# HGRN heads: gate projections in pieces of two contraction tiles, and another order between heads

## The chip, the cores and the metric

The kernel runs on one core of a Trainium2 chip. The metric is device time in microseconds (us) for one execution. TensorE multiplies matrices into PSUM, which has eight banks; VectorE and ScalarE read the banks and work on SBUF; SyncE and GpSimd start the transfers of weights and constants. Each engine runs its own queue of instructions in order and waits on semaphores that the others raise.

## The reference

Two transformer blocks on 1024 tokens and 256 context tokens, 1024 wide, in float32. The edited stage is the HGRN branch of block 1, a gated linear recurrence in two directions with 4 heads of 128:

```python
def _hgrn_direction(q, f_logit, inp, lb, s0, reverse):
    f = lb + (1.0 - lb) * jax.nn.sigmoid(f_logit.astype(jnp.float32))
    log_f = _heads(jnp.log(f), HG_HEADS, HG_DIM)
    k = _heads(1.0 - f, HG_HEADS, HG_DIM)
    v = _heads(inp, HG_HEADS, HG_DIM)
    ...
    o, s = _gla_chunkwise(q, k, v, log_f, s0)

def _gla_chunkwise(q, k, v, log_f, s0):      # chunks of 32 tokens
    cum = jnp.cumsum(log_f, axis=3)
    u = jnp.einsum('bhnck,bhncv->bhnkv', k * jnp.exp(cum_last - cum), v)
    def step(state, inp):
        d, un = inp
        return d[..., None] * state + un, state
    ...
    qd = chunks(q) * jnp.exp(cum)
    scores = jnp.einsum('bhnck,bhnsk->bhncs', qd, k * jnp.exp(-cum))
    scores = jnp.where(lower_tri, scores, 0.0)
    o = (jnp.einsum('bhncs,bhnsv->bhncv', scores, v)
         + jnp.einsum('bhnck,bhnkv->bhncv', qd, s_start))
    ...
def _hgrn_readout(o, g_raw, norm_w, dtype):
    y = _rmsnorm(o, norm_w) * jax.nn.silu(g)
```

The gate logits of both directions, the query and the output gate are projections of the normalized tokens, each with a contraction over 1024.

## The kernel before, in words

The program is written out by hand, engine by engine; what stands in an engine's function is its order, and nothing schedules it anew. The stage is `hgrn`. It takes the heads one after the other.

**Fills.** A head needs ten projections, called fills (`fills`, n = 0 to 9). Fills 0 to 5 are the gates (`FG` is 6): two directions, each 256 context tokens and twice 512 tokens, so fills 0 and 3 are 256 wide and the others 512. Fills 6 and 7 are the query's two halves, 8 and 9 the output gate's. Each fill has eight contraction tiles (`KT` is 8), summed in one PSUM bank by `project` (L1590; the matmul is L1603). ScalarE's `store` empties the bank: gates with a sigmoid (L1680), query and output gate with a SiLU (L1682). `ps_full` counts fills that are done, `ps_free` fills that are stored. Float32 matmuls appear as two records each in the trace.

**Operands.** VectorE turns the sigmoids into forget gates (L1749), ScalarE takes their logarithms (L1703), VectorE sums them in chunks of 32 with a scan (L1755), ScalarE takes two exponentials (L1706, L1707), and VectorE makes the keys, the decays and the scaled query (L1759 to L1766). `q_rd` says that the operands stand; `chunks(h)` on TensorE waits for it.

**Steps.** `chunks(h)` (L1607) has 22 steps, s = 0 to 21, one for each tile of 128 tokens and direction, and two to finish. In step s TensorE transposes keys of tile s (L1616, bank 4), multiplies the keys of tile s-1 with the values (the updates, L1629, banks 0 to 3), makes the scores of tile s-1 (L1635, bank 5, from tile 4 on) and the outputs of tile s-2 (L1648, L1651, bank 6). ScalarE copies the turned keys out (L1717). VectorE advances the state four times (L1785), one after the other, masks the scores (L1797) and copies the outputs (L1806, L1809). The updates of a tile wait for the state of the tile before (`s_rd`).

**Gates ahead.** While head h is in its steps, TensorE also projects the gates of head h+1. `beside` says in which: one whole fill at the end of steps 2, 5, 8, 11, 14 and 17, always in bank 7. Head 1's first four gate fills are projected before head 0's steps. The other four fills of head h+1 follow after the last step. Then come the transposes of the head's normalized outputs (L1660), and the next head's steps.

**Between heads.** ScalarE sums the squares of the outputs (L1695), takes logarithm and exponential for the root (L1725, L1726), stores fills 6 and 7 of the next head, and then takes the logarithms of its gates. VectorE scales the outputs (L1811), makes the forget gates, and goes on to the scans; `gated` (L1740) multiplies the turned outputs with the output gate. A change between sigmoid, SiLU, logarithm and exponential puts a table load on ScalarE.

Of the kernel before, what the change touches and what calls it, by code (L numbers as in the profile page):

```python
# [20 lines left out]
P = 128  # L21
# [1497 lines left out]
def hgrn(pg):  # L1519
# [40 lines left out]
    r_sq = pg.shared_sem("norm_squares", HEADS * T // P)  # L1560
# [3 lines left out]
    AHEAD = FH + 4  # L1564

    def bank_of(h, n):

        if FH * h + n < AHEAD:
            return (f0 + FH * h + n) % 8
        return 7 if n < FG else 2 + n - FG  # L1570

    def beside(h):

        todo = range(AHEAD - FH if h == 0 else 0, FG)
        return {3 * i + 2: n for i, n in enumerate(todo)}
# [13 lines left out]
    def tensor(e):  # L1589
        def project(h, which):  # L1590
            for n in which:
                part, (t, a, b) = fills[n]
                f = f0 + FH * h + n
                if f < f0 + AHEAD:
                    pg.bank_free(e, f)
                elif n < FG:
                    e.wait_ge(pg.ps_free, f)
                elif n == FG:
                    e.wait_ge(s_rd, 20 * h)
                    e.wait_ge(sm_rd, 16 * h)  # L1600
                slot = pg.weights(e, g0 + 2 * h + part)
                for k in range(KT):
                    mm = e.matmul(pg.ps[:, bank_of(h, n), 0:b - a], slot[:, (2 * k + t) * P:(2 * k + t + 1) * P],  # L1603
                                  h1[:, k, a:b], start=(k == 0), stop=(k == KT - 1))
                mm.then_inc(pg.ps_full, 1)

        def chunks(h):  # L1607
            e.wait_ge(pg.ps_free, f0 + max(FH * (h + 1), AHEAD))
            e.wait_ge(q_rd, 2 * h + 2)
            for s in range(2 * NT + 2):  # L1610
                if s < 2 * NT:
                    k, d = divmod(s, 2)
                    t = tile_of(k, d)
                    if h or s:
                        e.wait_ge(k_cp, 20 * h + s)
                    e.transpose(pg.ps[:, 4, 0:P], A[:, 2 * (h % 2) + d, t * P:(t + 1) * P], pg.ident).then_inc(t_rd, 1)  # L1616
                if 1 <= s <= 2 * NT:
# [9 lines left out]
                    for c in range(4):  # L1627
                        r = slice(C * c, C * c + C)
                        mm = e.matmul(pg.ps[:, c, 0:P], KT_[r, E % 4, :], V[r, t, h * P:(h + 1) * P], start=True, stop=True)  # L1629
                    mm.then_inc(u_rd, 1)  # L1630
                    if k >= 2:
                        L = 16 * h + u - 4
                        if L:
                            e.wait_ge(sm_rd, L)
                        e.matmul(pg.ps[:, 5, 0:P], Cn[:, d, t * P:(t + 1) * P], B[:, d, t * P:(t + 1) * P],  # L1635
                                 start=True, stop=True).then_inc(sc_rd, 1)
                if s >= 2:
# [3 lines left out]
                    if k >= 2:  # L1641
# [3 lines left out]
                        if L:  # L1645
                            e.wait_ge(o_cp, L)
                        bank = pg.ps[:, 6, 0:P]
# [10 lines left out]
            r_sc.wait(e, h + 1)  # L1658
            for t in range(T // P):
                mm = e.transpose(pg.ps[:, t // 4, (t % 4) * P:(t % 4 + 1) * P], YT[:, t, :], pg.ident)  # L1660
            mm.then_inc(y_turned.sem, 1)

        project(0, range(FH))
        project(1, range(AHEAD - FH))
# [3 lines left out]
    def scalar(e):  # L1668
# [28 lines left out]
        store(0, range(FH))  # L1697
        for h in range(HEADS):
            if h:
                store(h, [FG + 1])  # L1700
# [7 lines left out]
            if h:  # L1708
                store(h, range(FG + 2, FH))
            else:  # L1710
                store(1, range(AHEAD - FH))
            for s in range(2 * NT):
# [5 lines left out]
                if h + 1 < HEADS and s - 1 in beside(h):  # L1718
                    store(h + 1, [beside(h)[s - 1]])
                if s - 4 >= 12:  # L1720
                    square(h, s - 4)
            for s in range(2 * NT - 4, 2 * NT):
# [3144 lines left out]
```

## Time and profile before

| | us |
|---|---|
| median of 3 runs | 3565.79 |
| lowest, highest | 3562.51, 3567.89 |
| span of the profiled execution | 3560.1 |
| HGRN stage in it, first projection to last gated output | 425.5 to 900.2 |

The profiled execution is a further one; its span runs from its first to its last instruction. In a timeline a row is a run of equal instructions: its start, how long it lasted, engine, line, operation, and in brackets the idle time of the engine before it and what ended it. `PE` is TensorE's matmuls, `DVE` VectorE, `ACT` ScalarE. The end of a matmul is modelled, so starts are the safer numbers. `PEclk` is the clock granted to TensorE, 1.00 for 2.4 GHz and 0.50 for 1.2 GHz.

### The profile page before, as it was taken

Reading aid. Unit: us, or ns where it says so; the run is one execution under the profiler, and the core shown is the slowest. Engines: PE = TensorE matmul, PEld = TensorE weight load, DVE = VectorE, ACT = ScalarE, POOL = GpSimd, SP = SyncE. Lnnn points to the kernel's source line nnn. Section 1 sums busy time; section 2 is a strip of 40 time slices with the busy share of each in tenths; the row PEclk is TensorE's granted clock in tenths of the full one; section 3 lists DMA queues with packets and bytes.
Section 4 is the critical chain, followed back from the end, with each engine's and each line's share of the span. In section 5 each row is a group of like instructions: output and inputs, shape, how many; then the busy total and the mean of one; then the engine's idle time right before and its main releaser. Section 6 shows DMA issues by size and latency. Waiting matters only on the chain. (4 is left out here: it accounts for less than half of the span.)

```text
span 3560.1 us, 38398 instructions
## 1 busy us (share of the span) xinstructions
PE 3274.5 (92%) x15060; PEld 2447.1 (69%) x15060; DVE 1885.4 (53%) x2863; ACT 1217.0 (34%) x1887; POOL 657.4 (18%) x616
## 2 busy tenths in 40 slices
PE   7999998988899999999998998888968899999997
PEld 4476544444678778888887777665456678888785
DVE  6546626446323374443476734445675376555558
ACT  3325623212422253333233333451220243333344
POOL 3100000000100025544001010001000015555433
PEclk8899999996899999999999999998989899999998
DMA  5430000000333232222766123233224133222765
GB/s 227 172 130 13 10 24 24 13 13 1 121 117 104 96 104 80 86 83 87 288 247 258 43 65 93 90 97 125 60 107 154 59 103 110 97 105 101 256 241 171
DMA packets 124763, 389.24 MB, mean 109 GB/s; under 512 B 15751, under 2 KB 33159, under 8 KB 109352
## 3 DMA queue, kind: packets, MB, share of 16 engines
q1 hardware_dynamic: 86872, 267.32, 21.8%
q0 software_dynamic: 21056, 111.05, 8.4%
q10 hardware_dynamic: 16656, 8.42, 1.3%
q8 instruction: 120, 1.97, 0.2%
q14 instruction: 59, 0.48, 0.0%
HBM read 312.17 MB, written 74.58 MB: 109 GB/s over the span
## 5 line engine op out<-in xcount | busy, mean ns | idle before, releaser
L1603 PE MATMUL banks<-work,weight_ring 128*128 128x512 f32 (+1 forms) x640 | 263.8, 573 | 0.5 <-ACTq L4685 0.5
L2185 POOL TENSOR_TENSOR quad_raw<-quad_raw 128x512 f32<-128x512 f32 x160 | 234.7, 1468 | 124.1 <-DMA quad_raw<-in_w_gu 117.9
L2317 PE MATMUL banks<-block_t_high,quad_low 128*128 128x512 f32 x608 | 236.5, 389 | 0.0
L1603 PEld LDWEIGHTS banks<-work,weight_ring 128*128 128x128 f32 x640 | 126.3, 200 | 129.2 <-issue 123.8
L1785 DVE SCALAR_TENSOR_TENSOR x<-x,work,banks 128x128 f32<-128x128 f32 x320 | 111.3, 348 | 137.9 <-PE banks L1629 127.4
L2470 ACT ACTIVATE quad_partial<-banks 128x512 f32<-128x512 f32 x160 | 95.6, 598 | 241.3 <-PE banks L2317 236.6
L2315 PE MATMUL banks<-block_t_high,quad_high_b 128*128 128x512 f32 x456 | 177.5, 389 | 0.2 <-ACT quad_partial L2470 0.2
L2316 PE MATMUL banks<-block_t_low,quad_high_b 128*128 128x512 f32 x456 | 177.4, 389 | 0.0
L2317 PE MATMUL banks<-block_b_high,quad_low 128*128 128x512 f32 x456 | 177.4, 389 | 0.0
L3331 PE MATMUL banks<-mix_high,ring_parts 128*128 128x512 f32 x320 | 135.0, 422 | 13.2 <-ACT work L3390 4.5
L2556 DVE TENSOR_TENSOR quad_gated<-banks,quad_partial 128x512 f32<-128x512 f32 x40 | 27.7, 692 | 214.8 <-PE banks L2317 211.2
L2661 PE MATMUL banks<-hidden_high,pair_high 128*128 128x512 f32 x352 | 137.4, 390 | 1.5 <-DVE x L2720 1.5
L2663 PE MATMUL banks<-hidden_high,pair_low 128*128 128x512 f32 x352 | 136.9, 389 | 0.0
L2662 PE MATMUL banks<-hidden_low,pair_high 128*128 128x512 f32 x352 | 136.9, 389 | 0.0
L2317 PEld LDWEIGHTS banks<-block_t_high,quad_low 128*128 128x128 f32 x608 | 114.2, 188 | 23.6
L3332 PE MATMUL banks<-mix_low,ring_parts 128*128 128x512 f32 x320 | 129.2, 404 | 0.0
L3333 PE MATMUL banks<-mix_high,ring_parts 128*128 128x512 f32 x320 | 128.9, 403 | 0.0
L2235 DVE TENSOR_TENSOR quad_low<-quad_raw,quad_high_a 128x1536 fp32r<-128x1536 f32 x44 | 84.9, 1928 | 77.5 <-POOL quad_raw L2185 76.1
L1872 POOL DMA_DIRECT2D branches<-work x32 | 17.4, 543 | 555.1 <-ACT work L1943 552.8
L2315 PE MATMUL banks<-block_b_high,quad_high_a 128*128 128x512 f32 x304 | 118.3, 389 | 0.0
L2316 PE MATMUL banks<-block_b_low,quad_high_a 128*128 128x512 f32 x304 | 118.3, 389 | 0.0
L2235 DVE TENSOR_TENSOR quad_low<-quad_raw,quad_high_b 128x2048 fp32r<-128x2048 f32 (+1 forms) x44 | 94.3, 2143 | 34.1 <-ACT quad_high_b L2224 34.1
(650 smaller groups left out, 8174.6 us busy)
## 6 DMA issues: line engine op xcount, KB each, us to landing
quad_raw<-in_w_gu SPq DMA_DIRECT2D x40, 768.0 KB, 4.3
condition_space<-in_mod_w POOLq DMA_DIRECT2D x24, 1024.0 KB, 6.9
pair_raw<-in_w_down SPq DMA_DIRECT2D x22, 1024.0 KB, 5.4
down_raw<-in_w_down SPq DMA_DIRECT2D x33, 512.0 KB, 4.5
columns_raw<-ffn_blocks SPq DMA_DIRECT2D x33, 512.0 KB, 5.6
weight_ring<-in_w_merge SPq DMA_DIRECT2D x24, 512.0 KB, 3.8
quad_raw<-in_w_gu SPq DMA_DIRECT2D x48, 256.0 KB, 3.1
weight_ring<-in_dft SPq DMA_DIRECT2D x12, 1024.0 KB, 5.0
```

The lines of the kernel that those rows point to most:

```text
L1603: mm = e.matmul(pg.ps[:, bank_of(h, n), 0:b - a], slot[:, (2 * k + t) * P:(2 * k + t + 1) * P], h1[:, k, a:b], start=(k == 0), stop=(k == ...
L2185: e.tensor_tensor(self.weight(n, out), self.weight(n, a), self.weight(n, b), op).then_inc(self.sums.sem, 1)
L2235: e.tensor_tensor(flat(pg.w_low[n % 2][:, a:b]), pg.w_raw[n % 2].big[:, a * HALF:b * HALF], flat(high).bitcast(F32), ALU.subtract).then_in ...
L2315: e.matmul(bank, w_hi[:, k], hi[:, k], start=(start and k == 0), stop=False, skip_group_check=again)
L2316: e.matmul(bank, w_hi[:, k], lo[:, k], start=False, stop=False, skip_group_check=again)
L2317: mm = e.matmul(bank, w_lo[:, k], hi[:, k], start=False, stop=(k == 3), skip_group_check=again)
L2661: e.matmul(bank, wh[:, k, m], hh[:, k], start=(p == 0 and k == 0), stop=False)
L2662: e.matmul(bank, wh[:, k, m], hl[:, k], start=False, stop=False)
L2663: mm = e.matmul(bank, wl[:, k, m], hh[:, k], start=False, stop=(p == NP - 1 and k == 1))
L3331: e.matmul(bank, w_hi[:, c], MH[:, k, t], start=start, stop=False)
L3332: e.matmul(bank, w_hi[:, c], ML[:, k, t], start=False, stop=False)
L3333: mm = e.matmul(bank, w_lo[:, c], MH[:, k, t], start=False, stop=stop)
```

## The change

It has four parts.

- **Gates in pieces.** `beside` becomes a list with one entry for each of the 22 steps: two contraction tiles of a 512-wide gate fill, or four of a 256-wide one, behind the outputs of the step. The six gate fills end with step 19. Steps 20 and 21 take four tiles each of fill 6.
- **The start.** Head 1's first four gate fills are no longer projected before head 0's steps, and `chunks` no longer waits for all stores.
- **Banks and order on TensorE.** Fill 6 goes to bank 4, fill 7 to bank 7, fills 8 and 9 to banks 5 and 6. The output transposes move between fill 7 and fill 8.
- **Between heads.** ScalarE takes the next head's gate logarithms right behind the logarithm of the root, ahead of the root's exponential, and stores fills 6 to 9 behind the exponentials. VectorE makes the next head's forget gates (and clears the first states) ahead of the scaling, and does `gated` of the last head ahead of the two query products.

```diff
-    AHEAD = FH + 4
+    BANK = (7, 7, 7, 7, 7, 7, 4, 7, 5, 6)
+    STEPS = 2 * NT + 2
...
-        todo = range(AHEAD - FH if h == 0 else 0, FG)
-        return {3 * i + 2: n for i, n in enumerate(todo)}
+    def in_steps():
+
+        out, finished = [], {}
+        for n in range(FG + 1):
+            _, (_, a, b) = fills[n]
+            each = 4 if n == FG or b - a < HALF else 2
+            for k in range(0, KT, each):
+                finished[n] = len(out)
+                out.append([(n, j) for j in range(k, k + each)])
+        return out, finished
+
+    beside, finished = in_steps()
...
+            for n, k in todo:
                 part, (t, a, b) = fills[n]
                 f = f0 + FH * h + n
...
+                if k == 0:
+                    if n == 0 and h:
+                        e.wait_ge(pg.ps_free, f - 2)
+                    elif n < FG and h == 0:
+                        if n >= 4:
+                            e.wait_ge(pg.ps_free, f - 3)
+                    elif 0 < n < FG:
+                        e.wait_ge(pg.ps_free, f)
+                    elif n == FG and h:
+                        e.wait_ge(k_cp, 20 * h)
+                    elif n == FG + 1 and h:
+                        e.wait_ge(pg.ps_free, f - 1)
+                    elif n == FG + 2 and h:
+                        e.wait_ge(sm_rd, 16 * h)
+                    elif n == FG + 3 and h:
+                        e.wait_ge(o_cp, 16 * h)
...
-            e.wait_ge(pg.ps_free, f0 + max(FH * (h + 1), AHEAD))
             e.wait_ge(q_rd, 2 * h + 2)
...
-                if h + 1 < HEADS and s in beside(h):
-                    project(h + 1, [beside(h)[s]])
+                if h + 1 < HEADS:
+                    project(h + 1, beside[s])
             if h + 1 < HEADS:
-                project(h + 1, range(FG, FH))
...
-        project(0, range(FH))
-        project(1, range(AHEAD - FH))
+                project(h + 1, all_of([FG + 1]))
+            turn_outputs(h)
+            if h + 1 < HEADS:
+                project(h + 1, all_of([FG + 2, FG + 3]))
+
+        project(0, all_of(range(FH)))
...
+        store(0, range(FG))
+        gate_logs(0)
+        for h in range(HEADS):
             for d in range(2):
                 e.wait_ge(c_rd, 2 * h + d + 1)
                 e.activation(Cn[:, d, :], B[:, d, :], ACT.Exp, scale=-1.0).then_inc(n_rd, 1)
                 e.activation(B[:, d, :], B[:, d, :], ACT.Exp).then_inc(e_rd, 1)
-            if h:
-                store(h, range(FG + 2, FH))
-            else:
-                store(1, range(AHEAD - FH))
+            store(h, range(FG, FH))
...
+                if h + 1 < HEADS:
+                    store(h + 1, [n for n in range(FG) if finished[n] == s - 1])
```

Three places show the new order. TensorE, from the end of head 0's tail into head 1's steps. Before (L1660 the output transposes, L1616 key transposes, L1629 updates, L1603 projection):

```order
L1603 MATMUL banks<-work,weight_ring 128x512 x32
L1660 MATMUL banks<-parameters,work 128x128 x8
L1616 MATMUL banks<-parameters,x 128x128 x2
L1629 MATMUL banks<-work,x 128x128 x4
L1616 MATMUL banks<-parameters,x 128x128
L1629 MATMUL banks<-work,x 128x128 x4
L1603 MATMUL banks<-work,weight_ring 128x256 x8
```

After (L1631 the output transposes, L1643 key transposes, L1656 updates, L1620 projection):

```order
L1620 MATMUL banks<-work,weight_ring 128x512 x12
L1631 MATMUL banks<-parameters,work 128x128 x8
L1620 MATMUL banks<-work,weight_ring 128x512 x16
L1643 MATMUL banks<-parameters,x 128x128
L1620 MATMUL banks<-work,weight_ring 128x256 x4
L1643 MATMUL banks<-parameters,x 128x128
L1656 MATMUL banks<-work,x 128x128 x4
L1620 MATMUL banks<-work,weight_ring 128x256 x4
L1643 MATMUL banks<-parameters,x 128x128
L1656 MATMUL banks<-work,x 128x128 x4
L1620 MATMUL banks<-work,weight_ring 128x512 x2
```

The transposes now stand inside the tail's projections, and a piece of projection stands in every step, from step 0 on.

ScalarE between heads 0 and 1. Before (L1725 and L1726 the root, L1682 the stores of query and output gate, L1703 the gate logarithms, L1706 and L1707 the exponentials):

```order
L1725 ACT_TABLE_LOAD
L1725 ACTIVATE work<-work,parameters 128x8
L1726 ACT_TABLE_LOAD
L1726 ACTIVATE work<-work 128x8
L1682 ACT_TABLE_LOAD
L1682 ACTIVATE work<-banks 128x512 x2
L1703 ACT_TABLE_LOAD
L1703 ACTIVATE work<-x 128x1280 x2
L1706 ACT_TABLE_LOAD
```

After (L1755 and L1759 the root, L1730 the gate logarithms, L1737 and L1738 the exponentials):

```order
L1755 ACT_TABLE_LOAD
L1755 ACTIVATE work<-work,parameters 128x8
L1730 ACTIVATE work<-x 128x1280 x2
L1759 ACT_TABLE_LOAD
L1759 ACTIVATE work<-work 128x8
L1737 ACTIVATE work<-work 128x1280
L1738 ACTIVATE work<-work 128x1280
```

The gate logarithms stand two table loads and two stores earlier; the four stores (L1712) follow together behind the exponentials.

VectorE at the same place. Before (L1811 the scaling, L1749 forget gates, L1755 scan):

```order
L1811 TENSOR_TENSOR work<-work 128x1024
L1749 TENSOR_SCALAR x<-x,parameters 128x1280 x2
L1755 SCALAR_TENSOR_TENSOR work<-work 128x1280
L1756 TENSOR_SCALAR x<-x 128x1280
```

After (L1780 forget gates, L1782 clearing, L1850 the scaling, L1791 scan):

```order
L1780 TENSOR_SCALAR x<-x,parameters 128x1280 x2
L1782 MEMSET x 128x128 x2
L1850 TENSOR_TENSOR work<-work 128x1024
L1791 SCALAR_TENSOR_TENSOR work<-work 128x1280
L1792 TENSOR_SCALAR x<-x 128x1280
```

The forget gates no longer stand behind the scaling, and with it behind the root.

## Rows read from the trace of the kernel before

**Rows 1.** Stretches: us, busy of PE, PEld, DVE, ACT, POOL, PEclk, DMA share, GB/s.
```profile
603.60:718.00 114.40, 99.27 (x540) 53.85 (x540) 54.54 (x132) 29.88 (x61) 0.00 (x0) 0.93 0.06 19
...
833.10:900.20 67.10, 53.42 (x380) 33.77 (x380) 39.95 (x119) 11.39 (x40) 0.00 (x0) 0.50 0.00 1
```

**Rows 2.** Timeline, TensorE, steps of head 1: start, us, work, [idle before].
```profile
668.48 0.50 PE L1629 MATMUL banks<-work,x 32*128 32x128 f32 x8 [0.45 <-ACT x L1717]
...
669.91 7.13 PE L1603 MATMUL banks<-work,weight_ring 128*128 128x512 f32 x16
...
677.08 0.50 PE L1629 MATMUL banks<-work,x 32*128 32x128 f32 x8
...
679.30 0.50 PE L1629 MATMUL banks<-work,x 32*128 32x128 f32 x8 [0.46 <-ACT x L1717]
```

**Rows 3.** Timeline, TensorE, end of head 1, starts of heads 2 and 3.
```profile
684.85 27.73 PE L1603 MATMUL banks<-work,weight_ring 128*128 128x512 f32 x64
712.42 1.04 PE L1660 MATMUL banks<-parameters,work 128*128 128x128 f32 x8
718.04 0.45 PE L1616 MATMUL banks<-parameters,x 128*128 128x128 f32 x1 [4.58 <-issue]
...
833.07 0.45 PE L1616 MATMUL banks<-parameters,x 128*128 128x128 f32 x1 [4.57 <-issue]
```

**Rows 4.** Timeline, ScalarE, between heads 1 and 2.
```profile
685.73 1.28 ACT L1725 ACT_TABLE_LOAD   x1
...
687.35 1.28 ACT L1726 ACT_TABLE_LOAD   x1
...
700.80 2.43 ACT L1703 ACTIVATE work<-x 128x1280 f32<-128x1280 f32 x2
```

**Rows 5.** Timeline, VectorE, between heads 1 and 2.
```profile
688.88 1.23 DVE L1811 TENSOR_TENSOR work<-work 128x1024 f32<-128x1024 f32 x1 [3.60 <-ACT work L1726]
690.02 1.80 DVE L1749 TENSOR_SCALAR x<-x,parameters 128x1280 f32<-128x1280 f32 x2
702.10 2.83 DVE L1755 TENSOR_TENSOR_SCAN work<-work 128x1280 f32<-128x1280 f32 x1 [10.28 <-ACT work L1703]
...
717.85 1.40 DVE L1740 SCALAR_TENSOR_TENSOR work<-banks,parameters,work 128x512 f32<-128x512 f32 x2
```

**Rows 6.** Timeline, start of the stage: ScalarE, TensorE.
```profile
460.15 0.60 ACT L1680 ACTIVATE x<-banks 128x512 f32<-128x512 f32 x1 [6.27 <-PE banks L1603]
...
508.69 0.33 PE L1616 MATMUL banks<-parameters,x 128*128 128x128 f32 x1 [0.47 <-ACT x L1680]
```

**Rows 7.** Timeline, all engines, a step early in head 1.
```profile
614.25 0.27 PE L1616 MATMUL banks<-parameters,x 128*128 128x128 f32 x1
...
614.56 0.28 ACT L1717 ACTIVATE x<-banks 128x128 f32<-128x128 f32 x1 [8.03 <-PE banks L1616]
614.86 1.28 ACT L1680 ACT_TABLE_LOAD   x1
614.89 0.33 PE L1616 MATMUL banks<-parameters,x 128*128 128x128 f32 x1
...
616.15 0.38 ACT L1680 ACTIVATE x<-banks 128x256 f32<-128x256 f32 x1
```

**Rows 8.** Busy time by stretch, columns as in rows 1.
```profile
757.00:760.00 3.00, 2.45 (x31) 1.75 (x32) 2.27 (x9) 0.28 (x1) 0.00 (x0) 0.99 0.01 3
760.00:763.00 3.00, 3.00 (x16) 2.12 (x16) 1.66 (x6) 0.00 (x0) 0.00 (x0) 0.50 0.03 5
763.00:766.00 3.00, 3.00 (x14) 2.42 (x13) 0.00 (x0) 0.00 (x0) 0.00 (x0) 0.94 0.00 0
```

**Rows 9.** Timeline, VectorE, two state steps of head 3.
```profile
862.37 1.50 DVE L1785 SCALAR_TENSOR_TENSOR x<-x,work,banks 128x128 f32<-128x128 f32 x4 [0.86 <-PE banks L1629]
...
865.25 1.50 DVE L1785 SCALAR_TENSOR_TENSOR x<-x,work,banks 128x128 f32<-128x128 f32 x4 [0.86 <-PE banks L1629]
```

**Rows 10.** Timeline, TensorE, the fourth gate fill within head 2's steps.
```profile
761.33 4.70 PE L1603 MATMUL banks<-work,weight_ring 128*128 128x256 f32 x16
```

More of the change, by code:

```diff
@@ L1589, in tensor, with project @@
     def tensor(e):
-        def project(h, which):
-            for n in which:
+        def project(h, todo):
+            for n, k in todo:
                 part, (t, a, b) = fills[n]
                 f = f0 + FH * h + n
[L1594 to L1600, printed above, removed]
-                slot = pg.weights(e, g0 + 2 * h + part)
[L1602 to L1605, printed above, removed]
+                if k == 0:
[14 more added lines that the diff above has]
+                        e.wait_ge(o_cp, 16 * h)
+                slot = pg.weights(e, g0 + 2 * h + part)
+                mm = e.matmul(pg.ps[:, bank_of(h, n), 0:b - a], slot[:, (2 * k + t) * P:(2 * k + t + 1) * P],
+                              h1[:, k, a:b], start=(k == 0), stop=(k == KT - 1))
+                if k == KT - 1:
+                    mm.then_inc(pg.ps_full, 1)
@@ L1607, in chunks, with all_of, turn_outputs @@
+        def all_of(which):
+            return [(n, k) for n in which for k in range(KT)]
+        def turn_outputs(h):
+            r_sc.wait(e, h + 1)
+            for t in range(T // P):
+                mm = e.transpose(pg.ps[:, t // 4, (t % 4) * P:(t % 4 + 1) * P], YT[:, t, :], pg.ident)
+            mm.then_inc(y_turned.sem, 1)
         def chunks(h):
-            e.wait_ge(pg.ps_free, f0 + max(FH * (h + 1), AHEAD))
             e.wait_ge(q_rd, 2 * h + 2)
-            for s in range(2 * NT + 2):
+            for s in range(STEPS):
@@ L1628, in chunks @@
                         r = slice(C * c, C * c + C)
-                        mm = e.matmul(pg.ps[:, c, 0:P], KT_[r, E % 4, :], V[r, t, h * P:(h + 1) * P], start=True, stop=True)
+                        mm = e.matmul(pg.ps[:, c, 0:P], KT_[r, E % 4, :], V[r, t, h * P:(h + 1) * P],
+                                      start=True, stop=True)
                     mm.then_inc(u_rd, 1)
@@ L1695, in square, with gate_logs @@
             e.activation(junk, YT[:, t, :], ACT.Square, accum_out=ss[:, t:t + 1]).then_inc(r_sq.sem, 1)
-        store(0, range(FH))
-        for h in range(HEADS):
-            if h:
-                store(h, [FG + 1])
+        def gate_logs(h):
             for d in range(2):
@@ L1742, in gated, with forget_gates @@
             ins.then_inc(done, 1)
-        for h in range(HEADS):
-            a = [A[:, 2 * (h % 2) + d, :] for d in range(2)]
+        def forget_gates(h):
             e.wait_ge(pg.ps_free, f0 + FH * h + FG)
@@ L1748, in vector @@
                 i = 4 * d + h
-                e.tensor_scalar(a[d], a[d], pg.one_minus_lb[:, i:i + 1], pg.lb[:, i:i + 1], ALU.mult,
-                                ALU.add).then_inc(f_rd, 1)
+                a = A[:, 2 * (h % 2) + d, :]
+                e.tensor_scalar(a, a, pg.one_minus_lb[:, i:i + 1], pg.lb[:, i:i + 1], ALU.mult, ALU.add).then_inc(f_rd, 1)
+            for d in range(2):
+                ch(e.memset(S[:, 8 * d, :], 0.0))
+        forget_gates(0)
+        for h in range(HEADS):
+            a = [A[:, 2 * (h % 2) + d, :] for d in range(2)]
             for d in range(2):
```

50 lines of the change are left out of this document (26 added, 24 removed).

## The prediction

> **What bounds the kernel now.** The busy table and the chain that ended last cannot answer this: the chain ends long after the edited stage. I read the stage cut at each head's first transpose, then the timelines of TensorE, ScalarE and VectorE inside one head, looking at each place for the wait that ends last. A middle head takes 114.4 us, of which TensorE is busy 99.3 at a mean granted clock of 0.93; the last head, without projections, runs at 0.50, the lower of the clock's two levels [rows 1]. Within a head two regimes alternate [rows 2]. A step with no projection is a loop between two engines: updates on TensorE, four chained state steps on VectorE, updates again. It takes 2.20 us and TensorE idles 0.46 of it (677.08 to 679.30). A step that carries a whole gate fill takes 8.60 us (668.48 to 677.08) and is all TensorE; VectorE idles there. So the idle 0.46 is never filled, since the next projection tile is behind a step boundary. Between heads there is a third regime. After the last outputs (684.85, call it E) TensorE projects four fills in 27.57 us, but the next head starts only at 718.04, E + 33.2 [rows 3]: ScalarE stores two query fills first, then loads the logarithm table, and takes the gates' logarithms at E + 15.95 [rows 4], and VectorE's scans start at E + 17.25 [rows 5]. TensorE has nothing to do for the last 4.6 us.
>
> **The start of the stage.** TensorE projects ten fills of head 0 and four of head 1 before the first chunk step at 508.69 [rows 6]. Now the first chunk waits for its ten alone. A wide fill is 27.57 / 4 = 6.89 us at full clock [rows 3], a narrow one half; the four that go are 6.89 x 2 + 3.45 x 2 = 20.7, and the 0.47 in which TensorE waited for the last store goes too. Head 0 then starts at 487.5, **21.2 us earlier**, if its operands are ready. They are: ScalarE has the sixth gate at 460.8 [rows 6], table, logarithm and scan put the scan at about 463.5, and 17.1 us after a scan starts (below) the operands stand, at about 481.
>
> **The steps.** Every step now carries two 512-wide tiles (four narrow ones), 4 x 0.43 = 1.72 us by 6.89 / 8 for each tile. The step with eight tiles took 8.60; six tiles fewer leave 8.60 - 5.17 = 3.43 us, one switch between small matmuls and projection included [rows 2, 3]. That is above the 2.20 of the loop, so TensorE sets the pace and does not idle. There are 14 such steps (6 to 19): 48.0 us. Steps 0 to 5 have no outputs: a transpose and updates are 0.64 us [rows 7], with the tiles 2.4; step 0 about 2.0, step 5 with its scores 2.7. Step 2 has a wait of its own. Fill 1 goes into bank 7, which ScalarE must have emptied of fill 0, and ScalarE's first sigmoid of a head needs a table load. In the trace the same copy, load and store stand at 614.56, 614.86 and 616.15: the next instruction could start about 2.2 us after the transpose at 614.25, where the tiles were due after 0.64 [rows 7]. So step 2 costs about 3.95. The later handovers of bank 7 are free: ScalarE's copy and a 0.60 store end about 1.1 us after a transpose, the tiles are due 1.6 after it (0.20, and then the 1.43 from 668.48 to 669.91 [rows 2]). Steps 0 to 5: 2.0 + 3 x 2.4 + 3.95 + 2.7 = 15.9. Step 20 has updates, scores, outputs and four tiles, 1.43 + 3.45 = 4.9, step 21 its outputs, 0.75. With the odd tenths of waits for semaphores I take **70.0 us** from a head's start to E.
>
> What the single bank costs is bounded below by nothing (all hidden) and above by the 1.6 at step 2 plus about 1 us at each of the five other handovers.
>
> The Trainium skill, page "Perfetto Trace Analysis", Optimizing Tensor Performance, Matmuls, speaks against this change there: independent matmul groups should rotate through different PSUM banks, so that the evacuation of one overlaps the next. By that rule all six handovers of a head are open, some 7 us in a head instead of 1.6. The rows agree with it for step 2 alone.
>
> **Between heads.** TensorE after E: the last four tiles of fill 6 (3.45), fill 7 (6.89), eight transposes (about 0.95), fills 8 and 9 (13.78): 25.1 us. The other engines: ScalarE loads the logarithm table at E + 0.88, and where it loaded the exponential's it now starts the gates' logarithms, E + 2.50, for 2.43 [rows 4]. VectorE's forget gates, put ahead of the scaling, take 1.80 [rows 5] and are ready by E + 2.3, under the first load. From the start of the second load to VectorE's scaling were 1.53 us (687.35 to 688.88); now that makes E + 6.46. It lasts 1.23, overlapping the next a little; the scans, now queued behind it, start at E + 7.6, not 17.25 [rows 5]. From the first scan to the operands were 15.75 us (702.10 to 717.85); the gated output of the head before, 1.40, now stands ahead of the two query products: 17.1, so operands at E + 24.7 and the head's start at E + 24.9. The two paths end within 0.2 us of each other; TensorE's is later, **25.1 in place of 33.2**. The output transposes need the scaling, done at E + 7.7, and are reached at E + 10.4: no wait. The query stores wait behind the exponentials until about E + 18, still ahead of the products that need them (E + 22.3). The last store (fill 9) delays the head's first key copy by about 0.4 us, under step 0's tiles. SyncE's loads keep their order, and each slot is free 25 us or more before its next use.
>
> **The sum.** A head is 70.0 + 25.1 = 95.1. Heads 0 to 2 from 487.5: head 3 starts at 772.8, where it started at 833.07 [rows 3]: 60.3 us earlier. Head 3 has no projection, and I let it take as long as before. Against the 60.3 stands the clock. Before, TensorE idles 4.6 us in front of a head [rows 3], and behind head 3's pause comes half clock [rows 1]; that pause goes, and the sum uses full-clock rows. But a head keeps one sparse place, the 1.6 us wait in step 2. After 757 to 760, where only small matmuls ran, the clock fell; from 760 to 763 it was at half, with small matmuls up to 761.33 and projection behind them, and from 763 it was 0.94 [rows 8, 10]. I allow 2.3 us for one or two such dips. **Forecast: 58 us less**, a span of 3502, and against the median of 3565.8 (5.7 above the span) 3507.8 us.
>
> **Rivals.** *The clock falls in the steps and stays down; slower.* A small-matmul step at half clock takes 2.88 us [rows 9], and two tiles there 3.44: 6.3 in place of 3.43, 2.9 more. It decides from about 20 of the 66 steps. If it starts in step 3 and lasts to E in all three heads, it costs 19 x 3 x 2.9 = 165, or about 150 us, since some steps hold less: 3658; in one head alone about 50, 3558. For it: in head 3 TensorE is busy without pause at half clock and the clock never rises, and its array now sees small matmuls for half of every step. Against it: the dip at 760 ended with such a mix [rows 8, 10]. 8%, of which 5% slower.
>
> The Trainium skill, page "TensorE: Matmul & The Clock Gate", section "HAM oscillation — how this bites in real kernels", asks for all contraction tiles of one output in one run, so that TensorE's clock stays up. That is a rule against splitting the contraction over the steps, and by it the time is this rival's, above 3600. The trace agrees only for steps without any projection.
>
> *The handovers are all open.* If ScalarE's stores come late at each, 5 x 1 us in three heads: +15, 3523. 8%.
>
> *Head 3 keeps full clock*, since no pause precedes it: 15 to 16 steps of 2.20 for 2.88, 10.5 us less: 3497. Against it: its first steps hold only small matmuls, and from 757 to 760 such steps brought the clock down [rows 8]. 7%.
>
> *The order between heads brings nothing*, because a wait that I don't see (the root's table, the scaling) holds the scans as long as before: 3 x 8 = 24 back, 3532. 4%.
>
> **The numbers.** The forecast has 73%, with its own range 3500 to 3516. The range 3494 to 3527 takes in open handovers and the fast head 3, and leaves 12% out. What a measurement of this kernel can tell from no change is about 0.2%, 7 us. Faster 0.92, same 0.03 (one head at half clock), slower 0.05.
>
> **What would show it.** Right: head 0's first chunk transpose near 487.5; updates 3.43 apart in steps 6 to 19; 95 us between heads' starts; scans 7.6 us after E; TensorE without a gap ahead of each head; one gap of 1.6 us in step 2; granted clock near 1.0 in heads 0 to 2. Wrong: a clock of 0.5 across steps with projection, updates 6.3 apart, gaps at each change of fill, or a pause of TensorE between the last fill and the next head.

## The result, and the profile after

| | before | after |
|---|---|---|
| median of the runs, us | 3566.84 (3562.51 to 3578.63, 4 runs) | 3506.81 (3504.79 to 3508.18, 4 runs) |
| span of the profiled execution, us | 3560.1 | 3506.1 |
| ratio of the times, 95% interval | 1 | 0.9827 (0.9806 to 0.9848) |
| heads' first transposes, us | 508.7, 603.6, 718.0, 833.1 | 487.7, 582.9, 678.1, 773.2 |
| end of the stage, us | 900.2 | 839.6 |
| from there to the end, us | 2659.8 | 2666.4 |

The changed kernel is faster by 60 us than the kernel before on the same chip. The forecast was 3507.8 us; the median is 3506.8.

The stretches of the profile after, cut at the heads' starts and at the stage's end as in [rows 1] (us; busy time of PE, PEld, DVE, ACT, POOL; granted clock; DMA share; GB/s):

```profile
487.69:582.87 95.18, 93.55 (x542) 49.42 (x540) 54.34 (x131) 25.79 (x58) 0.00 (x0) 1.00 0.07 23
582.87:678.05 95.18, 93.55 (x542) 49.42 (x541) 54.43 (x131) 25.80 (x58) 0.00 (x0) 1.00 0.07 23
678.05:773.22 95.17, 93.54 (x541) 49.42 (x540) 54.35 (x131) 25.80 (x58) 0.00 (x0) 1.00 0.03 12
773.22:839.60 66.38, 52.17 (x381) 33.09 (x379) 38.44 (x115) 11.87 (x41) 0.00 (x0) 0.53 0.00 1
839.60:3506.00 2666.40, 2481.02 (x11068) 1980.08 (x11068) 1403.95 (x1801) 909.93 (x1304) 594.68 (x499) 0.96 0.36 125
```

A middle head took 114.40 us with TensorE busy 99.27 at a clock of 0.93 [rows 1]. Now it takes 95.18 with TensorE busy 93.55 at 1.00. The matmuls are the same, so of the 19.2 us 5.7 were busy time, lost to the lower clock, and 13.5 were idle time. The last head, which has no projection beside it, is nearly as it was: clock 0.53 (0.50 before), 66.4 us to the end of the stage (67.1 before).

The same stretch from the stage's end to the kernel's end in the profile of before, same columns:

```profile
900.20:3560.00 2659.80, 2473.43 (x11068) 1973.20 (x11068) 1408.20 (x1801) 909.87 (x1304) 598.69 (x499) 0.96 0.37 125
```

It has the same instructions (11068 matmuls) and took 6.6 us less. That is why the two spans are 54 us apart and the stage 60.6. It isn't a cost of the change: the changed kernel profiled a second time (below) took 2657.6 there.

The stage's first fill, before and then after. Before, 14 fills stand ahead of head 0's first transpose at 508.69 [rows 6]; after, ten stand ahead of 487.69:

```profile
425.47 82.75 PE L1603 MATMUL banks<-work,weight_ring 128*128 128x256 f32 x224 [0.52 <-ACTq L4685]
425.75 62.11 PE L1620 MATMUL banks<-work,weight_ring 128*128 128x256 f32 x160 [0.52 <-ACTq L4724]
```

From its first fill to head 0 the stage took 83.2 us before and takes 61.9 now, 21.3 less. The whole stage, from its first fill, took 474.7 us and takes 413.8, 60.9 less.

TensorE in the first steps of head 0, and three steps with outputs (start, us, work, [idle before]), against [rows 2, 6, 7]:

```profile
487.69 0.27 PE L1643 MATMUL banks<-parameters,x 128*128 128x128 f32 x1
487.80 1.89 PE L1620 MATMUL banks<-work,weight_ring 128*128 128x256 f32 x8
...
492.20 0.50 PE L1656 MATMUL banks<-work,x 32*128 32x128 f32 x8
494.33 1.98 PE L1620 MATMUL banks<-work,weight_ring 128*128 128x512 f32 x4 [1.63 <-ACT x L1710]
...
507.40 0.50 PE L1656 MATMUL banks<-work,x 32*128 32x128 f32 x8
...
508.83 1.98 PE L1620 MATMUL banks<-work,weight_ring 128*128 128x512 f32 x4
...
510.86 0.50 PE L1656 MATMUL banks<-work,x 32*128 32x128 f32 x8
```

Updates (L1656) are 3.45 us apart, and TensorE does not idle: every such step has the same shape, where before one step of 8.60 us followed on steps of 2.20. The only gap is in step 2, where fill 1 waits for ScalarE's copy out of bank 7 (L1710). It is the only one in each of the three heads with projection: a head's 95.18 us less 93.55 of busy time is 1.63. The line of costly groups on the profile's page says the same, since 3 x 1.63 = 4.9; the other 0.5 of its 5.4 us stands in front of the stage's first fill:

```profile
L1620 PE MATMUL banks<-work,weight_ring 128*128 128x512 f32 (+1 forms) x640 | 265.0, 560 | 5.4 <-ACT x L1710 4.9
```

Between heads 0 and 1, TensorE, then VectorE, then ScalarE, against [rows 3, 5, 4]. The last outputs end at E = 557.86:

```profile
557.86 10.57 PE L1620 MATMUL banks<-work,weight_ring 128*128 128x512 f32 x24
568.26 1.04 PE L1631 MATMUL banks<-parameters,work 128*128 128x128 f32 x8
569.13 13.90 PE L1620 MATMUL banks<-work,weight_ring 128*128 128x512 f32 x32
582.87 0.27 PE L1643 MATMUL banks<-parameters,x 128*128 128x128 f32 x1
```

```profile
558.20 1.80 DVE L1780 TENSOR_SCALAR x<-x,parameters 128x1280 f32<-128x1280 f32 x2
...
564.27 1.23 DVE L1850 TENSOR_TENSOR work<-work 128x1024 f32<-128x1024 f32 x1 [3.88 <-ACT work L1759]
565.41 2.82 DVE L1791 TENSOR_TENSOR_SCAN work<-work 128x1280 f32<-128x1280 f32 x1
...
580.20 2.35 DVE L1805 SCALAR_TENSOR_TENSOR work<-work 128x1024 f32<-128x1024 f32 x2
```

```profile
558.73 1.28 ACT L1755 ACT_TABLE_LOAD   x1
560.03 0.30 ACT L1755 ACTIVATE work<-work,parameters 128x8 f32<-128x8 f32 x1
560.24 2.41 ACT L1730 ACTIVATE work<-x 128x1280 f32<-128x1280 f32 x2
562.67 1.28 ACT L1759 ACT_TABLE_LOAD   x1
```

TensorE works without a gap from the last outputs to the next head's first transpose, E + 25.0, where it stood still for the last 4.6 us of 33.2 [rows 3]. The logarithms (L1730) share the root's table and need no load of their own, and the scans start at E + 7.55 instead of E + 17.25 [rows 5]. VectorE has the operands at 582.55, 0.3 before TensorE is done with its projection: the two paths end together.

### The profile page after: what moved, and what is told of

The parts are those of the page before. It is cut to its first block and busy times, and to the rows that moved or that the text cites. A ratio compares the mean times of both kernels' runs of the same rounds, so it can differ in the third digit from the quotient of the medians.

```text
span 3506.1 us, 38398 instructions
## 1 busy us (share of the span) xinstructions
PE 3262.6 (93%) x15060; PEld 2438.4 (70%) x15060; DVE 1879.7 (54%) x2863; ACT 1203.9 (34%) x1878; POOL 653.3 (19%) x616
## 5 line engine op out<-in xcount | busy, mean ns | idle before, releaser
L1620 PE MATMUL banks<-work,weight_ring 128*128 128x512 f32 (+1 forms) x640 | 265.0, 560 | 5.4 <-ACT x L1710 4.9
L1620 PEld LDWEIGHTS banks<-work,weight_ring 128*128 128x128 f32 x640 | 115.9, 190 | 115.0 <-issue 104.5
L2951 PE MATMUL banks<-down_high 128*128 128x512 f32 x264 | 103.9, 394 | 6.8 <-DVE down_low L3023 3.6
```

The source lines that it names most:

```text
L2951: e.matmul(bank, wh[:, c], bh, start=first, stop=False)
```

## The experiments

Every ratio is to the kernel before on the same chip, with its 95% interval. What runs ahead of the stage differs by some us between executions: head 0 starts at 485.7 to 490.2 in kernels with the same beginning, and at 482.2 and 482.6 in two more, though in each of these the stage's first fill is 61.9 us ahead of it. So I compare lengths: the stage from head 0's first transpose to the gated output of head 3 (351.9 us in the changed kernel), a head's cycle (95.18), from its start to E (70.2 to 70.3) and from E to the next start (25).

### Whole fills again, the rest of the change kept

Six gate fills of the next head go whole into steps 2, 5, 8, 11, 14 and 17; each is stored one step later.

```
-        out, finished = [], {}
+        out, finished = [[] for _ in range(STEPS)], {}
-        for n in range(FG + 1):
-            _, (_, a, b) = fills[n]
-            each = 4 if n == FG or b - a < HALF else 2
-            for k in range(0, KT, each):
-                finished[n] = len(out)
-                out.append([(n, j) for j in range(k, k + each)])
+        for n in range(FG):
+            finished[n] = 3 * n + 2
+            out[finished[n]] = [(n, j) for j in range(KT)]
+        for i in range(2):
+            out[2 * NT + i] = [(FG, j) for j in range(4 * i, 4 * i + 4)]
...
-            if h + 1 < HEADS:
-                store(h + 1, [FG - 1])
```

> The changed kernel (3506.8 us) with one part undone: the gate fills are whole again, in steps 2, 5, 8, 11, 14 and 17, in bank 7; the early start and the order between heads stay. Theory (the pieces fill TensorE's idle time in every step): a group of three steps takes 13.0 us instead of 3 x 3.46 = 10.4, so a head's way to its last outputs grows from 70.1 us to 81 to 84, +33 to +42 in three heads: 3540 to 3549. Rival (the gain is that of the start and of the order between heads, since TensorE was 87% busy in a middle head anyway): +15 at most, under 3522.

Measured: 3536.13 us (3535.74 to 3540.77), 0.9904 (0.9883 to 0.9924), 4 us under the range expected. The stage took 388.2 us, 36.3 more than with the pieces, which was expected; from a head's start to E it was 81.8, 80.5 and 84.9 us, against 70.2. The three heads, and TensorE over one period of three steps in head 1:

```profile
485.71:592.43 106.72, 96.88 (x542) 52.86 (x540) 54.34 (x131) 25.70 (x58) 0.00 (x0) 0.97 0.06 20
592.43:697.79 105.36, 95.52 (x541) 51.76 (x540) 54.41 (x131) 25.70 (x58) 0.00 (x0) 0.98 0.06 21
697.79:807.53 109.74, 99.89 (x541) 54.52 (x540) 54.44 (x131) 25.70 (x58) 0.00 (x0) 0.94 0.03 10
```

```profile
642.53 7.13 PE L1618 MATMUL banks<-work,weight_ring 128*128 128x512 f32 x16
...
654.12 0.50 PE L1654 MATMUL banks<-work,x 32*128 32x128 f32 x8 [0.45 <-ACT x L1743]
...
655.55 7.13 PE L1618 MATMUL banks<-work,weight_ring 128*128 128x512 f32 x16
```

A period of three steps takes 13.02 us (642.53 to 655.55). Three steps of the changed kernel take 10.35, but they hold six tiles of 512 columns and the period holds eight, which by 0.86 us a tile is 1.72 of the difference; so the two are not to be compared as they stand, as the expectation does. The loop's latency is the rest: in the two steps without projection TensorE waits 0.45 us in front of the updates. A whole head has the same matmuls in both kernels. There TensorE idles 9.8 us instead of 1.6 (in head 1, 5.0 in four waits for VectorE's states, 4.1 in nine for the key copies), which makes 24.6 us in three heads. The rest, a third of the 36.3, is the clock, which dips six times, each time beginning between two whole fills or before a head's first: TensorE's busy time is 3.3, 2.0 and 6.4 us longer than in the changed kernel, 11.7 of the 36.3. So the pieces are worth 29 us by the medians (27 by the ratios) and 36 by the stage, and they pay by giving each step something to do, not by less work.

### Logarithms behind the exponential and two query stores, as before

```
-            store(h, range(FG, FH))
+            store(h, range(FG + 2 if h else FG, FH))
...
-            if h + 1 < HEADS:
-                gate_logs(h + 1)
             e.wait_ge(r_lg, h + 1)
             e.activation(ss, ss, ACT.Exp, scale=-0.5).then_inc(r_rt.sem, 1)
+            if h + 1 < HEADS:
+                store(h + 1, [FG, FG + 1])
+                gate_logs(h + 1)
```

> The changed kernel with ScalarE's order between heads undone: root's logarithm, root's exponential, stores of fills 6 and 7, and only then the gates' logarithms; all else stays. Theory (VectorE's scans wait for these logarithms and then set the next head's start): the scans start near E + 13.6 instead of E + 7.6 (E is the end of the last outputs), the next head at E + 31 instead of E + 25; 3 x 5.8 = +17, and TensorE's pause of 5 to 6 us in front of each head brings half clock in its first steps, up to 4 us each: 3524 to 3537. Rival (TensorE's own path of 25.1 us hides them): 0 to +3, at most 3510.

Measured: 3527.17 us (3519.48 to 3532.34), 0.9877 (0.9853 to 0.9901); the stage took 374.4 us, 22.5 more. TensorE in front of head 1 (E = 560.35), and VectorE's first scan:

```profile
571.63 13.90 PE L1620 MATMUL banks<-work,weight_ring 128*128 128x512 f32 x32
591.38 0.47 PE L1643 MATMUL banks<-parameters,x 128*128 128x128 f32 x1 [5.85 <-DVE work L1806]
591.64 3.62 PE L1620 MATMUL banks<-work,weight_ring 128*128 128x256 f32 x8
```

```profile
574.17 2.83 DVE L1792 TENSOR_TENSOR_SCAN work<-work 128x1280 f32<-128x1280 f32 x1 [8.50 <-ACT work L1730]
```

The scan is at E + 13.8, the head's start at E + 31.0 instead of 25.0. The pause also triggers something: the clock is at half from 589.0 and again from 691.4, for 6.8 us each (the eight matmuls in 3.62 us, against 1.89 in the changed kernel), and heads 1 and 2 are about 2 us longer to E. The cycles are 6.0, 8.2 and 7.8 us longer, and the pause is 6.0 of each. The two parts, 36.3 + 22.5 = 58.8 us, come near to the 60.9 by which the whole stage is shorter.

### Four fills of head 1 ahead of the first head

They use banks 0 to 3, as head 0's did, and their stores stand ahead of head 0's first key copy, as before the change; `chunks(0)` waits for all stores again (these edits are left out below).

```
         project(0, all_of(range(FH)))
+        project(1, all_of(range(4)))
...
-                    project(h + 1, beside[s])
+                    project(h + 1, [v for v in beside[s] if h or v[0] >= 4])
```

> The changed kernel with the start undone: head 1's first four gate fills are projected before head 0's steps again (banks 0 to 3), and steps 0 to 11 of head 0 carry no projection. Theory (a step without projection cannot take less than the 2.2 us of the loop between TensorE and VectorE, so work taken out of the steps gives back only part): start +21.2, steps 0 to 5 about -4, steps 6 to 11 6 x (3.46 - 2.20) = -7.6, together +9 to +10, with a dip of the clock up to +14: 3516 to 3521. Rival (the early start is worth its whole 21 us): 3528.

Measured: 3523.65 us (3514.56 to 3527.39), 0.9865 (0.9842 to 0.9888). That is 2.7 us over the range expected. The first chunk starts at 507.37, and head 0 is shorter only by 3.7 us, so the stage, from its first fill, is 17.6 us longer. The expectation takes 11.6 us off head 0, which makes 58.6 us to E; it took 66.6. The 17.6 can't be added to the 36.3 and 22.5 of the two runs above, since the four fills moved here are pieces in head 0's steps too. The stretches of head 0:

```profile
507.37:509.80 2.43, 1.35 (x11) 0.72 (x11) 0.84 (x3) 0.83 (x3) 0.00 (x0) 1.00 0.00 0
509.80:543.90 34.10, 28.71 (x188) 17.39 (x189) 19.57 (x61) 2.77 (x10) 0.00 (x0) 0.50 0.00 1
543.90:598.87 54.97, 54.97 (x279) 27.02 (x278) 34.67 (x68) 18.80 (x39) 0.00 (x0) 1.00 0.06 20
```

```profile
540.37 3.74 PE L1622 MATMUL banks<-work,weight_ring 128*128 128x512 f32 x4
```

Steps 0 to 11 hold small matmuls alone. TensorE fell to the lower clock 2.4 us into them, was busy 28.71 of 34.10 us there, and came back to the upper clock at 543.9, within the first two projection tiles (from 540.37). So work done ahead is not free even where it only moves: here it left twelve steps to the lower clock, and the step that brought it back is one with projection.

Small matmuls alone don't bring the clock down everywhere, though. Head 0 of the kernel before has no projection behind step 5 either, and there such steps kept the upper clock for 33 us, after the whole fill in step 5:

```profile
540.00:550.00 10.00, 7.78 (x94) 5.09 (x94) 8.01 (x28) 1.39 (x5) 0.00 (x0) 1.00 0.04 13
550.00:560.00 10.00, 8.22 (x97) 5.34 (x97) 8.20 (x28) 1.40 (x6) 0.00 (x0) 1.00 0.01 2
```

So the same steps stand at both levels in these traces. The clock fell at the start of a head that has nothing but small matmuls there, in steps without scores and outputs, in which TensorE waits 1.3 to 1.5 us for VectorE; but it fell in later steps too, at 760 in the trace before [rows 8] and at 748 in the run with whole fills, where it held in the rows above. What decides between these, no run shows.

### Pauses put into the steps

To try the slower rival, ScalarE holds the key copy back once in each of heads 0 to 2, by 26 small copies, so that TensorE stands still in the middle of steps with two tiles.

```
+                if h < 3 and s == 7 + h:
+                    for _ in range(26):
+                        pg.achain(e)(e.activation(junk, pg.ident, ACT.Copy))
                 e.activation(KT_[:, E % 4, :], pg.ps[:, 4, 0:P], ACT.Copy).then_inc(k_cp, 1)
```

> The changed kernel with a pause of TensorE put into the steps of heads 0, 1 and 2: ScalarE does 26 idle copies ahead of the key copy of step 7, 8 and 9, about 9 us of work of which 3 are hidden, so TensorE stands still for about 6 us in each. Theory (half of each step is dense projection, and that brings the clock back): behind each pause the clock falls to half and is back within about 10 us, which costs 2 to 5 us: 3506.8 + 3 x 6 + 3 x 3.5 = 3535 (3528 to 3545). Rival (with small matmuls in half of each step the clock stays down until the head's tail): 12 steps x 2.9 = 35 us more in each head, 3625 or more.

Measured, in one run: 3527.65 us, beside 3571.08 of before (median of that chip). One run is not enough to judge the time (it lies just under the range expected), but the trace answers the question. TensorE behind the pause of head 0, and the stretches with their clocks:

```profile
515.13 0.47 PE L1643 MATMUL banks<-parameters,x 128*128 128x128 f32 x1 [5.89 <-ACT x L1748]
...
518.01 3.00 PE L1620 MATMUL banks<-work,weight_ring 128*128 128x512 f32 x4
...
522.48 1.98 PE L1620 MATMUL banks<-work,weight_ring 128*128 128x512 f32 x4
```

```profile
513.30:520.10 6.80, 4.97 (x24) 2.89 (x25) 1.89 (x6) 1.90 (x7) 0.00 (x0) 0.50 0.00 0
520.10:530.00 9.90, 9.90 (x80) 6.13 (x80) 4.94 (x17) 1.32 (x4) 0.00 (x0) 1.00 0.01 2
```

The clock fell to half in each pause and was back 6.8, 10.2 and 6.8 us after it fell. It never stayed down: a head cost 8.3 to 9.4 us more, of which the pause is 5.9. The rival that gives 3558 to 3658 us needs it to stay down for whole heads, and is refuted for steps of this shape, half small matmuls and half projection. Together with the run above: once down, the clock stayed at half for 34 us without the projection tiles, and for 7 to 10 with them.

### Another bank for the first fill

The trace shows one handover of bank 7 that is not hidden, the first of a head. Here fill 0 goes into bank 5, whose other user (the scores) comes later.

```
-    BANK = (7, 7, 7, 7, 7, 7, 4, 7, 5, 6)
+    BANK = (5, 7, 7, 7, 7, 7, 4, 7, 5, 6)
...
-                        e.wait_ge(pg.ps_free, f - 2)
+                        e.wait_ge(pg.ps_free, f - 1)
...
-                    elif 0 < n < FG:
+                    elif 1 < n < FG:
...
-                            e.wait_ge(pg.ps_free, f0 + FH * h + FG + 3)
+                            e.wait_ge(pg.ps_free, f0 + FH * (h + 1) + 1 if h + 1 < HEADS else f0 + FH * h + FG + 3)
```

> The changed kernel with fill 0 of the next head in bank 5 instead of 7: bank 5 is first used by the scores of step 5, so fill 1 can start in bank 7 in step 2 without waiting for the table load and the store of fill 0. Theory: the only wait of TensorE in a head, 1.63 us in step 2, goes, 3 x 1.63 = 4.9 us less than the changed kernel's 3506.8: 3502 (3500 to 3504). Rival (another wait takes its place: the key copy of step 3 stands behind the table load too, and TensorE needs it in step 4): no change, 3506 to 3508.

Measured: 3498.03 us (3489.66 to 3503.26), 0.9803 (0.9785 to 0.9821). TensorE at the same place, where the changed kernel waits 1.63 us:

```profile
493.52 0.50 PE L1656 MATMUL banks<-work,x 32*128 32x128 f32 x8
493.95 1.98 PE L1620 MATMUL banks<-work,weight_ring 128*128 128x512 f32 x4
```

The wait is gone, a head's cycle is 93.48 instead of 95.18, and nothing else came late in its place: 3 x 1.70 = 5.1 us in the stage. The stage took 346.5 us, 5.4 less. By the ratios the whole is 8.6 us below the changed kernel's, though the two did not run side by side; 4.9 were expected, and the stage shows 5.4.

### Head 3 kept at the upper clock by extra matmuls

Head 3 gets matmuls that compute nothing anyone reads, into bank 7, where the other heads have their projection. They are work on top of the reference's.

```
                 if h + 1 < HEADS:
                     project(h + 1, beside[s])
+                else:
+                    for n in (512, 256) if s < 5 else (128,):
+                        e.matmul(pg.ps[:, 7, 0:n], pg.ident, h1[:, 0, 0:n], start=True, stop=True)
```

> The changed kernel with idle matmuls in head 3, which has no projection (identity times tokens, into bank 7, read by nobody): a 512-wide and a 256-wide one in steps 0 to 4, a 128-wide one in each later step. Theory (head 3 runs at half clock only because its first steps leave TensorE idle for most of the time): the clock stays at its upper level, steps take 2.2 to 2.3 us instead of 2.88, and the merge behind starts at full clock: 10 to 13 us less, 3494 to 3497. Rival (small matmuls bring the clock down whatever stands between them): the clock falls, and the idle matmuls cost up to 0.3 us a step: 3507 to 3513.

Measured: 3502.0 us (3493.63 to 3508.15), 0.9807 (0.9791 to 0.9824). Head 3 of the changed kernel after its first 4.2 us, and head 3 with the extra matmuls:

```profile
777.40:839.60 62.20, 50.19 (x361) 32.02 (x360) 36.92 (x111) 10.55 (x37) 0.00 (x0) 0.50 0.00 1
```

```profile
775.64:824.40 48.76, 42.71 (x427) 27.68 (x425) 34.26 (x112) 9.82 (x38) 0.00 (x0) 1.00 0.01 1
```

With more matmuls on TensorE (427 in 48.76 us) the head is shorter: 46.9 us from its start to its last outputs instead of 57.7. The mechanism works, and the stage is 10.8 us shorter (341.1). But the time is not: against the changed kernel it is 5 us less by the medians, with intervals that overlap, where 10 to 13 were expected. The stages behind it took 2674.8 us in this execution, the slowest of its five. The expectation also wanted the next stage to start at full clock. It does not: TensorE waits 4.8 us for the scaled outputs behind the head, and the clock falls again, at 824.4, before the stage ends at 831.2:

```profile
824.40:831.20 6.80, 1.97 (x8) 1.56 (x8) 2.61 (x3) 2.05 (x4) 0.00 (x0) 0.50 0.00 0
```

Which of the extra matmuls are needed was not tried. The matmuls of the later steps have 128 columns, no more than the head's own, and head 0 of before kept the upper clock in such steps with none added, so the wider ones of steps 0 to 4 may be enough.

### Both together

Both edits in one kernel.

> Both edits together, bank 5 for fill 0 and idle matmuls in head 3. Theory: the gains add, 15 to 18 us less than the changed kernel: 3489 to 3492. Rival: one of the two brings nothing, 3494 to 3503.

Measured: 3499.43 us (3487.34 to 3501.77), 0.9802 (0.9783 to 0.9822). The stage took 336.0 us, 15.9 less than the changed kernel's, nearly both savings added (5.4 + 10.8); the time is that of bank five alone, 3498.03 beside it, where 3489 to 3492 were expected: the rival's 3494 to 3503 came.

### The three once more, side by side

The changed kernel, bank five and both again, on one chip.

> The changed kernel, unaltered, timed beside the next two on the same chip, since runs of one kernel spread by 5 to 15 us in the stages behind the edited one. Its stage took 414 us (425.5 to 839.6) in the first profile; it should do so again within 0.5, with 70.3 us to the last outputs of heads 0 to 2, 24.9 to the next start, and 57.6 in head 3. Total 3500 to 3510.

> Fill 0 in bank 5, again. Theory: the stage is 4.9 us shorter than the changed kernel's in the same job, and so is the total within the spread of the later stages (2 to 8 less). Rival: what the stage gains is lost again in the later stages whatever the kernel, total the same.

> Fill 0 in bank 5 and idle matmuls in head 3, again. The stage is 15.5 us shorter than the changed kernel's. Theory (the later stages took 8 us longer in two profiles by the chance of where the clock dips fell): the later stages take 2661 to 2669 us as in the other kernels and the total is 12 to 16 less than the changed kernel's. Rival (the edit itself lengthens the later stages): they take 2672 or more again and the total is 5 to 9 less.

| | median (range), us | ratio (95%) | stage, us | behind the stage, us |
|---|---|---|---|---|
| changed kernel | 3504.38 (3498.30 to 3506.93) | 0.9826 (0.9812 to 0.9840) | 351.8 | 2657.6 |
| bank five | 3494.35 (3492.99 to 3498.17) | 0.9801 (0.9788 to 0.9814) | 346.6 | 2664.8 |
| both | 3493.21 (3491.82 to 3497.62) | 0.9798 (0.9785 to 0.9812) | 336.0 | 2671.2 |

The rest of the kernel in the three profiles, in that order:

```profile
840.10:3497.70 2657.60, 2471.75 (x11068) 1974.63 (x11068) 1408.38 (x1802) 909.79 (x1304) 595.67 (x499) 0.96 0.36 125
```

```profile
828.80:3493.60 2664.80, 2480.15 (x11068) 1979.67 (x11068) 1403.20 (x1801) 910.59 (x1304) 595.48 (x499) 0.96 0.37 125
```

```profile
818.60:3489.80 2671.20, 2481.77 (x11068) 1977.62 (x11068) 1409.24 (x1802) 910.26 (x1304) 596.09 (x499) 0.96 0.36 125
```

The stage repeats to 0.1 us. What lies behind it does not: the same 11068 matmuls are busy 2471.75 to 2481.77 us. Bank five is the better version by 10.0 us of median here (its interval and the changed kernel's just touch) and by 8.6 us by the ratios of the first runs; 5.2 of them are shown, in the stage. The rest is not the edit's as far as the profiles show: of the two profiled executions bank five's is 4.0 us shorter, with 6.1 less ahead of head 0, 5.2 less in the stage and 7.2 more behind it. Of the 10.6 us that the extra matmuls save in head 3, 1.1 arrive. In the three profiles with them the rest took 2671.2, 2673.6 and 2674.8 us, in the other four of the changed stage (after, its repeat and twice bank five) 2657.6 to 2666.4, and in the first four runs above up to 2669.5. So most of that gain was given back behind the stage. It is not lost at once: in the first 908 us behind the stage TensorE gets equally far in the three profiles of the table (3874 to 3882 matmuls in their records). What gives it back is open: the granted clock there is the same 0.96 in all three, TensorE's busy time is longer by 1.6 us, of 6.4, from bank five to both, and I tried nothing on it. The last run's result lies between its theory and its rival: the total is 11.2 us less than the changed kernel's, where 12 to 16 and 5 to 9 were said. As the kernel to keep I would take bank five alone: both is not distinguishable from it and carries dead work.

## Why the prediction was right

- **The start of the stage.** Said: head 0 at 487.5, 21.2 us earlier. Came: 487.69, and 21.3 less from the stage's first fill. The 21.2 was worked out and is right. That head 0 starts at 487.69 itself is luck, since the stage began at 420.3 to 428.2 in other executions of kernels with this beginning.
- **The steps.** Said: 3.43 us each in steps 6 to 19, the time of six tiles fewer. Came: 3.45, with TensorE without a gap. The run with whole fills shows that this part carries 36 us of the stage's 60.9, 25 of them idle time and 12 the clock's, which the prediction has only in that its sum uses full-clock rows.
- **Step 2 and bank 7.** Said: a wait of 1.6 once a head, the five later handovers free, from when ScalarE's copy and store end. Came: 1.63, and 4.9 in all three heads. Putting fill 0 elsewhere took 1.70 from a head, so the single bank costs that and no more. The rival "all handovers open", and with it the rule of the Trainium skill (page "Perfetto Trace Analysis", Optimizing Tensor Performance, Matmuls) to rotate the banks, holds here for the one group whose evacuation stands behind a table load. At the other five handovers the trace shows no wait with a single bank: 1.6 us of other matmuls lie between.
- **From a head's start to E.** Said: 70.0. Came: 70.2. **Between heads.** Said: 25.1, scans at E + 7.6, operands at E + 24.7. Came: 25.0, E + 7.55, and VectorE's last product ends at 582.55 = E + 24.7. The cycle of 95.1 came as 95.18.
- **The clock in heads 0 to 2.** The term that was off in size: I allowed 2.3 us for one or two dips behind the wait of step 2. There was none, in either profile of the changed kernel. The stretch from 757 to 760 in the trace before, from which I drew the allowance, was not a step with one wait of 1.6, but a run of steps without projection [rows 8]. With head 3's 0.7 us this is about the difference between the 58 said and the 60.9 that came.
- **Head 3.** Said: as long as before. Came: 57.7 us from its start to its last outputs, 58.4 before. The absent pause did not keep the clock up: it fell 4.2 us into the head, as the reasoning against that rival had it. The heads that begin with small matmuls alone (head 3 here, head 0 with four fills done ahead) fell after 4.2 and 2.4 us, with no more than 0.5 us of idle time in front of the head. But the reasoning was too simple: small matmuls alone kept the upper clock for 33 us in head 0 of before, a row that the prediction did not use. The two places it rests on are the first steps of head 3 and those at 757, and it takes them for the rule.
- **The clock stays at half in the steps.** Refuted by the pauses: 7 to 10 us at half clock each. The prediction put this rival beside the Trainium skill (page "TensorE: Matmul & The Clock Gate", section "HAM oscillation — how this bites in real kernels") as a rule against splitting a contraction. That reads too much into it: the page advises to run all contraction tiles of one output together for loops with thin outputs, in which TensorE stands idle for a transfer between the tiles. Here the splitting fills idle time. Whole fills in one run cost 36 us of the stage and gave the lower mean clock (0.94 to 0.98, against 1.00); between them lie steps with no projection at all.
- **The total.** Said: the stage 60.3 us shorter, and 58 with the allowance for the clock; came: 60.9 from first fill to end. The median is 1.0 us from the forecast. That is luck as far as it is nearer than the method can claim: the rest of the kernel, untouched, took 6.6 us more in the profile after and 2.2 less in its repeat, and I had no term for that beyond the 0.2%.

## What to carry to other kernels

Where small steps with a fixed latency alternate with blocks of dense work, cut the dense work so that each step gets a piece that is longer than the latency: here 0.45 us and more of idle time a step went, and the clock held, without any instruction being saved. Between two such loops, follow each engine's queue to the one operation that the next loop waits for longest (here the scans, behind two stores and a table load) and put that one first. And cost a single buffer by when its reader is done against what is queued in between, handover by handover; here one of six cost anything.

## What the hardware showed that I had not expected

- The same steps of small matmuls stood at either clock. Entered at half they stayed there for 34 us in head 0 with fills done ahead, though TensorE was busy 28.71 of 34.10 us, and rose 3.5 us into two projection tiles; entered at full behind a whole fill, they kept it for 33 us in head 0 of before. With pauses of 5.9 us in mixed steps the half clock lasted 6.8 to 10.2 us.
- Adding useless matmuls to a latency-bound stretch made it 10.8 us shorter (57.7 to 46.9), since the state loop itself runs through TensorE's small matmuls, and these ran at the upper clock. Of 10.6 us in the runs side by side 1.1 reached the total, which I can't explain.
- Untouched stages differ by 8.8 us between two profiles of one kernel (2657.6 and 2666.4), while the edited stage repeats to 0.1. For differences under 10 us the stage's own length is the measure to trust, and the total only says whether it arrives.
